# A two-block transformer layer on one core: latent attention's unrotated queries and keys made with features on partitions, and eight gate steps placed inside the attention

## The reference

```python
cq = rmsnorm_2(q_lat, q_norm_g[l])                       # 512 x 384
qb = (cq @ w_uq[l]).reshape(B, S, MLA_HEADS, MLA_QK_DIM) # 8 heads x 96
q_nope, q_rope = jnp.split(qb, [MLA_NOPE_DIM], axis=-1)  # 64 unrotated, 32 rotated
q_rope = apply_rope(q_rope, cos_b, sin_b)
ckv = rmsnorm_2(kv_lat, kv_norm_g[l])                    # 512 x 256
kvb = (ckv @ w_ukv[l]).reshape(B, S, MLA_HEADS, MLA_NOPE_DIM + MLA_V_DIM)
k_nope, vb = jnp.split(kvb, [MLA_NOPE_DIM], axis=-1)
k_rope = apply_rope(k_r[:, :, None, :], cos_b, sin_b)[:, :, 0, :]   # one 32-wide part for all heads
o_b = mla_attention(q_nope, q_rope, k_nope, k_rope, vb)  # causal softmax attention
y = sigmoid(g_a) * (o_a @ w_o_swa[l]) + sigmoid(g_b) * (o_b @ w_o_mla[l])
```

## Time and profile before

| | |
|---|---|
| median of three runs | 1228.16 us |
| the profiled execution's own time | 1228.82 us |
| its span in the trace | 1226.6 us |
| PE busy / DVE / ACT / POOL | 1203.6 / 630.9 / 542.0 / 513.6 us |
| granted TensorE clock | 0.998 of full speed |
| DMA engines' share | 28.9% |

### The profile page before, as it was taken

One profiled execution on the slowest core, in us unless ns is written; L12 is line 12 of the kernel. 1 busy time (PEld: TensorE's weight loads), 2 busy tenths in 40 slices (PEclk: granted clock), 3 DMA queues, 4 the chain that ended last, 5 costly groups with the idle time before them and its releaser, 6 DMA issues.

```text
span 1226.6 us, 15784 instructions
## 1 busy us (share of the span) xinstructions
PE 1203.6 (98%) x5888; PEld 999.9 (82%) x5888; DVE 630.9 (51%) x1489; ACT 542.0 (44%) x971; POOL 513.6 (42%) x279
## 2 busy tenths in 40 slices
PE   9999999999999999999999999999999999999997
PEld 8878788888888888699878878788888888888886
DVE  5789765774437284974855685855222231230003
ACT  6443573476523354534855476434323232231112
POOL 1428362454443424035353693443444434434441
PEclk9999999999999999999999999999999999999999
DMA  8205552202322522133012202333232332323221
GB/s 272 91 14 154 156 173 73 99 2 103 117 76 88 183 82 99 60 126 124 15 52 91 70 35 97 110 104 103 82 102 92 103 103 93 103 79 120 99 74 68
DMA packets 70842, 119.18 MB, mean 97 GB/s; under 512 B 5608, under 2 KB 33128, under 8 KB 70384
## 3 DMA queue, kind: packets, MB, share of 16 engines
q1 hardware_dynamic: 70768, 118.19, 28.9%
HBM read 107.67 MB, written 4.21 MB: 91 GB/s over the span
## 4 chain that ended last, share of the span: by engine, by line
PE 89%; DVE 4%; POOL 2%; ACT 2%; issue 1%; DMA 1%; SPq 1%; ACTq 0%; DVEq 0%; POOLq 0%
PE bank L1647 67%; PE bank L1968 9%; PE bank L1735 2%; PE bank L1703 2%; PE bank L1779 2%; PE bank L1717 2%; PE bank L1679 2%; POOL w_lo L678 1%; DVE tmp L1434 1%; PE bank L1818 1%; POOL w_lo L661 1%; ACT w_hi L781 1%; DVE xT L1436 0%; DVE sc L1183 0%; DMA w_raw<-in_w_in 0%
## 5 line engine op out<-in xcount | busy, mean ns | idle before, releaser
L661 POOL TENSOR_TENSOR w_lo<-w_raw,w_hi 128x2048 fp32r<-128x2048 f32 (+4 forms) x82 | 365.3, 4454 | 582.5 <-ACT w_hi L748 529.0
L1647 PE MATMUL bank<-aH,w_hi 128*128 128x512 f32 x800 | 318.7, 398 | 2.4 <-DVE mx L1183 0.8
L1647 PE MATMUL bank<-aH,w_lo 128*128 128x512 f32 x800 | 312.2, 390 | 0.0
L1647 PE MATMUL bank<-aL,w_hi 128*128 128x512 f32 x800 | 312.0, 390 | 0.0
L748 ACT ACTIVATE w_hi<-w_raw 128x2048 fp32r<-128x2048 f32 (+4 forms) x78 | 143.9, 1846 | 259.7 <-PE bank L1647 161.3
L1647 PEld LDWEIGHTS bank<-aH,w_hi 128*128 128x128 f32 x800 | 150.7, 188 | 32.0 <-issue 3.3
L1647 PEld LDWEIGHTS bank<-aH,w_lo 128*128 128x128 f32 x800 | 150.1, 188 | 32.2
L1647 PEld LDWEIGHTS bank<-aL,w_hi 128*128 128x128 f32 x800 | 150.6, 188 | 26.6 <-issue 0.2
L1106 DVE TENSOR_TENSOR fg<-bank,rB 128x512 f32<-128x512 f32 x22 | 15.1, 691 | 128.2 <-PE bank L1647 128.2
L1647 PE MATMUL bank<-w_hi,aH 128*128 128x512 f32 (+4 forms) x224 | 77.7, 347 | 2.2 <-ACT aH L991 1.9
L1647 PE MATMUL bank<-uH,w_hi 128*128 128x512 f32 x192 | 75.1, 391 | 1.7 <-DVE uL L1538 1.7
(11 more groups left out here) (313 smaller groups left out, 2132.7 us busy)
## 6 DMA issues: line engine op xcount, KB each, us to landing
w_raw<-in_w_in SPq DMA_DIRECT2D x23, 1024.0 KB, 4.9
w_raw<-in_w_gate SPq DMA_DIRECT2D x22, 512.0 KB, 3.6
w_raw<-in_w_up SPq DMA_DIRECT2D x22, 512.0 KB, 4.5
w_raw<-in_w_down SPq DMA_DIRECT2D x11, 1024.0 KB, 4.8
w_raw<-in_w_merge SPq DMA_DIRECT2D x8, 1024.0 KB, 4.8
w_raw<-in_w_out SPq DMA_DIRECT2D x8, 1024.0 KB, 4.9
w_raw<-in_w_ple_gate SPq DMA_DIRECT2D x4, 1024.0 KB, 4.8
w_raw<-in_w_in SPq DMA_DIRECT2D x4, 512.0 KB, 7.2
```

The lines of the kernel that those rows point to most:

```text
L661: pool.tensor_tensor(out=w_lo[:, c % 2, 0:n], in0=w_raw[:, c % 2, 0:n], in1=w_hi[:, c % 2, 0:n].bitcast(F32), op=ALU.subtract).then_inc(w_ ...
L1647: ins = pe.matmul(o, l, r, start=(kk == 0 and m == 0), stop=(kk == total - 1 and m == 2), skip_group_check=True)
```

## The change

The columns of the two weight matrices are gathered by kind instead of by group of heads. `uqn` makes the unrotated 64 features of all 8 heads with features on partitions (weights stationary, 36 matmuls of 512 columns; a bank holds two heads), `uqr` the 32 rotated ones with tokens on partitions (36 of 256 columns), `ukn` the unrotated keys with features on partitions (24 of 512), `ukv` the values (24 of 512). ACT copies the two halves of a bank of `uqn` or `ukn` to two heads of `mqT` or `mkT`. The rotated queries are turned by two groups of four transposes (`t.mq`, four heads in each), the shared rotated key by four (`t.kr`); DVE copies them to rows 64 to 96. The key's rotated rows are split once for both buffers of `mK` and stay there. DVE rotates all eight heads in one pass.

Each such weight chunk is loaded by one DMA per row block of 128, with runs of 64 floats (256 bytes) or 32 floats (128 bytes).

Eight of the 16 gate steps ahead of the attention go into it: one in every step from i = 2 to 25, then one from i = 27 and two from i = 33. ACT and POOL split the weights of `n3` at later steps. On POOL the second chunk of `n2` is split after the first two heads and no longer ahead of them.

```diff
-        unit(f"uq{i}", QR, 3, [("w_uq_2", 384 * i, 384)])
-    for i in range(2):
-        unit(f"ukv{i}", KVR, 2, [("w_ukv_2", 512 * i, 512)])
+    unit("uqn", QR, 3, [("w_uq_2", 0, DH)], H)
+    unit("uqr", QR, 3, [("w_uq_2", DH, MR)], H)
+    unit("ukn", KVR, 2, [("w_ukv_2", 0, DH)], H)
+    unit("ukv", KVR, 2, [("w_ukv_2", DH, DH)], H)
...
-SIDE_FIRST = {"fox": 8, "dsa": 8, "swa": 10, "mla": 16}
-SIDE_TAIL = {"fox": ((29, 2),), "dsa": ((29, 2),), "swa": ((25, 1), (35, 2)), "mla": ((22, 1),)}
-SIDE_HI = {"fox": (20, 27), "dsa": (20, 27), "swa": (16, 24), "mla": (11, 19)}
+SIDE_FIRST = {"fox": 8, "dsa": 8, "swa": 10, "mla": 8}
+SIDE_TAIL = {"fox": ((29, 2),), "dsa": ((29, 2),), "swa": ((25, 1), (35, 2)), "mla": ((27, 1), (33, 1))}
+SIDE_HI = {"fox": (20, 27), "dsa": (20, 27), "swa": (16, 24), "mla": (19, 27)}
...
-           "swa": ((16, 17, 18, 19), (24, 25, 26, 27)), "mla": ((12, 13, 16, 17), (20, 21, 24, 25))}
+           "swa": ((16, 17, 18, 19), (24, 25, 26, 27)), "mla": ((20, 21, 22, 23), (28, 29, 30, 31))}
...
-    for u in ("uq", "ukv"):
-        fill(f"{u}0", four); fill(f"{u}1", [4, 5, 6, 7])
-    fill("t.mq0", [0, 3, 4, 5]); fill("t.mk0", [6, 7, 0, 3])
-    fill("t.mq1", [4, 5, 6, 7]); fill("t.mk1", [0, 3, 4, 5])
+    fill("t.kr", [6]); fill("uqn", four); fill("uqr", [4, 5, 6, 7])
+    fill("ukn", four); fill("t.mq", [0, 3]); fill("ukv", [4, 5, 6, 7])
...
-                for arr, r0, c0, w, off in ps:
+                for arr, r0, c0, w, off, heads in ps:
+                    if heads > 1:
+                        for k in range(per):
+                            rows = dram[arr][0, r0 + k * P:r0 + (k + 1) * P, :].rearrange("p (h d) -> p h d", h=heads)
+                            sp_.dma_start(v[:, k, :].rearrange("p (h d) -> p h d", h=heads),
+                                          rows[:, :, c0:c0 + w]).then_inc(w_landed[c % 2], 16)
+                        continue
...
-                    t, m_ = ((mqT, mQ), (mkT, mK))[p]
+                    t, m_, n = ((mqT, mQ, MQK), (mkT, mK, DH))[p]
                     pool.wait_ge(mla_hi_ready, 2 * h + p + 1)
-                    pool.tensor_tensor(out=m_[0:MQK, h % 2, 1, :], in0=t[0:MQK, h, :],
-                                       in1=m_[0:MQK, h % 2, 0, :].bitcast(F32), op=ALU.subtract).then_inc(mla_lo_ready, 1)
+                    pool.tensor_tensor(out=m_[0:n, h % 2, 1, :], in0=t[0:n, h, :],
+                                       in1=m_[0:n, h % 2, 0, :].bitcast(F32), op=ALU.subtract).then_inc(mla_lo_ready, 1)
...
-            lo_through(UNITS["n2"][0] + 1)
+            lo_through(UNITS["n2"][0])
             for h in range(2):
                 split_head(h)
+            lo_through(UNITS["n2"][0] + 1)
             scale_rows("mla", sc2)
...
-                ahead(f"uq{i}")
-                for b in range(NB):
-                    evac(f"uq{i}", b, uq[i][:, b, :], src=bank_of(f"uq{i}", b)[:, 0:QR])
-            for i in range(2):
-                ahead(f"ukv{i}")
-                for b in range(NB):
-                    src = bank_of(f"ukv{i}", b)[:].rearrange("p (h d) -> p h d", h=4)
-                    wait_filled(act, f"ukv{i}", b)
-                    act.activation(mk[i][:, b, :, 0:DH], src[:, :, 0:DH], ACT.Copy).then_inc(mk_ready, 1)
-                    act.activation(mvS[:, b, 4 * i:4 * i + 4, 0, :], src[:, :, DH:2 * DH], ACT.Copy).then_inc(split_hi, 1)
+            for u, t in (("uqn", mqT), ("ukn", mkT)):
+                ahead(u)
+                for j in range(NB):
+                    wait_filled(act, u, j)
+                    act.activation(t[0:DH, 2 * j, :], bank_of(u, j)[0:DH, :], ACT.Copy)
+                    empties(act.activation(t[0:DH, 2 * j + 1, :], bank_of(u, j)[DH:P, :], ACT.Copy), u, j)
+                if u == "uqn":
+                    ahead("uqr")
+                    for b in range(NB):
+                        evac("uqr", b, uqR[:, b, :], src=bank_of("uqr", b)[:, 0:H * MR])
+            ahead("ukv")
+            for b in range(NB):
+                wait_filled(act, "ukv", b)
+                act.activation(mvS[:, b, :, 0, :], bank_of("ukv", b)[:].rearrange("p (h d) -> p h d", h=H),
+                               ACT.Copy).then_inc(split_hi, 1)
             hi_through(UNITS["n2"][0] + 1)
-            for i in range(2):
-                for j in range(4):
-                    evac(f"t.mk{i}", j, mkT[0:MQK, 4 * i + j, :], src=bank_of(f"t.mk{i}", j)[0:MQK, :])
-            wait_emptied(act, "t.mq1", 3)
             exps("mla", sc2, pT2, low_rows2)
...
-                    kr = kvl[:, b, KVR:KVR + MR].rearrange("p (o d) -> p o d", o=1).broadcast_to([P, 4, MR])
-                    ins = dve.tensor_copy(mk[i][:, b, :, DH:MQK], kr)
-                ins.then_inc(kr_copied, 1)
+            evac("t.kr", 0, krS[DH:MQK, :], src=bank_of("t.kr", 0)[0:MR, :])
             for j in range(NB):
                 gate_tile("n1", j, gates2[NB + j])
+            for b in range(NB):
+                wait_emptied(dve, "uqr", b)
+            rope_blocks(uqR[:, :, :].rearrange("p b (h d) -> p b h d", h=H), H, 16, "3", rp3)
+            wait_emptied(dve, "t.kr", 0)
             for i in range(2):
-                for b in range(NB):
-                    wait_emptied(dve, f"uq{i}", b)
-                uq4 = uq[i][:, :, :].rearrange("p b (h d) -> p b h d", h=4)
-                rope_blocks(uq4[:, :, :, DH:MQK], 4, 16, "3", rp3)
+                dve.tensor_copy(mK[DH:MQK, i, 0, :], krS[DH:MQK, :]).then_inc(kr_split, 1)
+            dve.wait_ge(kr_split, 2)
             for i in range(2):
-                for b in range(NB):
-                    splits[0] += 1
-                    dve.wait_ge(split_hi, splits[0])
-                    src = bank_of(f"ukv{i}", b)[:].rearrange("p (h d) -> p h d", h=4)
-                    empties(dve.tensor_tensor(out=mvS[:, b, 4 * i:4 * i + 4, 1, :], in0=src[:, :, DH:2 * DH],
-                                              in1=mvS[:, b, 4 * i:4 * i + 4, 0, :].bitcast(F32), op=ALU.subtract), f"ukv{i}", b)
-            for i in range(2):
-                for j in range(4):
-                    evac(f"t.mq{i}", j, mqT[0:MQK, 4 * i + j, :], src=bank_of(f"t.mq{i}", j)[0:MQK, :])
-                if i == 0:
-                    wait_emptied(dve, "t.mq0", 3)
-                    wait_emptied(dve, "t.mk0", 3)
-                    for h in range(2):
-                        split_head(h)
-            wait_emptied(dve, "t.mk1", 3)
+                dve.tensor_tensor(out=mK[DH:MQK, i, 1, :], in0=krS[DH:MQK, :], in1=mK[DH:MQK, i, 0, :].bitcast(F32),
+                                  op=ALU.subtract).then_inc(kr_split, 1)
+
+            def q_rope(h):
+                wait_filled(dve, "t.mq", h // 4)
+                ins = dve.tensor_copy(mqT[DH:MQK, h, :], bank_of("t.mq", h // 4)[MR * (h % 4):MR * (h % 4) + MR, :])
+                if h % 4 == 3:
+                    empties(ins, "t.mq", h // 4)
+                else:
+                    ins.then_inc(q_roped, 1)
+
+            for h in range(2):
+                q_rope(h)
+            for h in range(2):
+                dve.wait_ge(q_roped, h + 1)
+                dve.wait_ge(kr_split, 4)
+                wait_emptied(dve, "uqn", h // 2)
+                wait_emptied(dve, "ukn", h // 2)
+                split_head(h)
+            for h in range(2, H):
+                q_rope(h)
+            for b in range(NB):
+                splits[0] += 1
+                dve.wait_ge(split_hi, splits[0])
+                empties(dve.tensor_tensor(out=mvS[:, b, :, 1, :], in0=bank_of("ukv", b)[:].rearrange("p (h d) -> p h d", h=H),
+                                          in1=mvS[:, b, :, 0, :].bitcast(F32), op=ALU.subtract), "ukv", b)
+            for j in range(NB):
+                wait_emptied(dve, "ukn", j)
+            for half in range(2):
+                wait_emptied(dve, "t.mq", half)
             softmax("mla", sc2, pT2, lambda h, b: tab("causal")[:, (3 - b) * P:4 * P], low_rows2, oB)
...
-            def turn_mq(i):
-                pe.wait_ge(roped, 6 + 2 * NB + i)
-                for j in range(4):
-                    turn_tile(f"t.mq{i}", j, lambda b: uq[i][:, b, j * MQK:(j + 1) * MQK], rows=MQK)
-
-            def turn_mk(i):
-                pe.wait_ge(kr_copied, 2)
-                pe.wait_ge(mk_ready, 4 * i + 4)
-                for j in range(4):
-                    turn_tile(f"t.mk{i}", j, lambda b: mk[i][:, b, j, :], rows=MQK)
-
-            gemm("uq0", cqH, cqL, True, u_from("t.cq", 0))
-            gemm("uq1", cqH, cqL, True)
-            gemm("ukv0", ckH, ckL, True, u_from("t.ck", 0))
-            gemm("ukv1", ckH, ckL, True)
-            turn_mq(0)
-            side("mla", 0, 4)
-            turn_mk(0)
-            side("mla", 4, 8)
-            turn_mq(1)
-            side("mla", 8, 12)
-            turn_mk(1)
-            side("mla", 12, 16)
-            for j in range(4):
-                wait_emptied(pe, "t.mk1", j)
+            pe.wait_ge(roped, 5 + 2 * NB)
```

(15 more changed lines are left out.)

30 lines of the change are left out of this document (12 added, 18 removed).

## The result

The changed kernel takes 1231.39 us (median of ten runs, 1229.89 to 1232.41) against 1228.28 us of the kernel before (ten runs, 1227.17 to 1230.22): a ratio of 1.0024, 95% interval 1.0015 to 1.0033. It is slower by 3.1 us, and the forecast of 1227.0 us was wrong, with its range too (1224.0 to 1230.8).

A forecast was written before the change was run, and what follows sets the result against it. TensorE, busy 98% of the span, was taken as the bound: its program plus waits. The last value product ending 1.25 us earlier moved the end equally, 1228.16 - 1.25 = 1226.9, given as 1227.0 us, range 1224.0 to 1230.8.

The forecast's parts named there:

- TensorE's work: Latent attention stage: matmul time about unchanged (23.4 to 23.5 us), fewer transposes, so TensorE loses 5.4 us of work.
- The chain ahead of the attention: Through ACT, POOL and DVE before the attention: waits of 5.7 us replace 5.4 us of transposes; ninth gate step at 685.95.
- because of POOL: Ninth gate step, ahead of the attention: held until 685.95 by POOL's low part of n2's second chunk, ending at 685.85.
- In the attention: Ninth gate step to last value product: eleven more gate steps (7.7 us) and 2.9 us of waits; ends 1.25 us earlier.
- 2.3 for the low part of the last head ahead of step 28: Within the attention: TensorE waits 2.3 us for POOL's low part of the last head, the largest of three waits summing 2.9.
- Behind the attention: After the last value product: three fewer gate steps gain nothing, as `zb0` starts 21.0 us later; the end moves 1.25 us.
- The wait of 1.10 becomes 3.1: Ahead of `zb0`, behind the attention: TensorE has 2.0 us less to do, so its wait grows from 1.10 to 3.1 us.
- Loads: Weight DMAs in runs of 128 and 256 bytes: hidden, cost 0; upper bound 1.5 us if short runs took twice the row.
- rival (c): Small weight loads take twice the row's time and come late: 1228.4 us; part of the 61%.
- (b): Inside the attention, POOL excludes DVE, delaying its casts and maxima, and POOL gets rows later: 1230.7 us, 12%.
- (d): Gate steps put into the attention only fill time POOL's pace left empty; 5.3 us of waits stay: 1229.3 us, within 61%.

The follow-up runs named there:

- layout alone: The changed kernel with the gate-step tables and POOL's order put back as before (16 gate steps ahead of the attention), only the new query and key layout left: 1224.57 us.
- both gaps filled: The changed kernel with 27 matmuls nobody reads put into TensorE's two gaps (ahead of first scores and ninth gate step, and ahead of step 27): 1228.04 us.
- the gates alone: The kernel before, old layout with 64 transposes, given only the changed kernel's gate steps, weight halves and quarters and POOL's order: 1234.52 us.

## Why the prediction was wrong

**TensorE's work**: right, in that TensorE is busy 5.0 us less in the layout alone for the 5.4 forecast. Of these, 2.7 are gained from S to V once enough work stands behind them. The layout alone gains 4.0 us, but the other 1.3 come behind V.

**The chain ahead of the attention**: right in nearly all its links. Counted from S, POOL's first chunk ends at 26.97 us (forecast 26.8), its second at 37.57 (37.45); the waits are 0.44, 0.48, 0.73 and 2.88 + 0.78 = 3.66, for 0.5, 1.0, 0.3 and 3.9. DVE is 1.0 late at bank 4; 0.6 of this are its six copies, each of which takes 4.29 / 6 = 0.72 instead of 0.62. That is not POOL's doing: the first copy of a rotated part, at 670.99, takes 0.67 while POOL is idle. So the third score tile waits for DVE's first maximum until the very moment at which POOL's second chunk ends, and the ninth gate step, which was to start "because of POOL", starts one tile of scores later. The cast of `mQ` that was to wait for POOL took 4.11 us, until 676.52; the one of `mK` behind it 0.41. What failed is the step from the waits to the time: "waits of 0.5 + 1.0 + 0.3 + 3.9 = 5.7 us have taken the place of the 5.4 us of transposes" prices a wait at its length. The forecast had the gap right and took the work behind it at full clock. The ninth gate step starts 38.70 us from S instead of 37.55, and from the third score tile on scores and gates run at 0.52 until 693.40.

**In the attention**: the sum of waits, 2.9, was right in size (3.09), and its place wrong. The step "2.3 for the low part of the last head ahead of step 28" named the wrong consumer: the gate step of 27 came to POOL's fourth quarter first. POOL's rows and the head's low part are only the next in line, as the run with gate steps from 29 shows (1.84 and 0.34). And it was one gap, not three small waits, so the clock fell a second time.

The two falls cost 3.4 us together by the medians (both gaps filled against the changed kernel) and 1.9 each when filled apart. The traces close the sum from S to V, where 5.3 us were missed. With both gaps filled the ninth gate step starts 38.88 us from S, of which 0.69 are the fill, so 38.19 without it: 0.64 over the forecast, DVE's lateness. From there to V are 68.51 us, against 37.55 to 105.85 = 68.30 in the forecast: 0.2 over, the size of the gap. The other 4.4 us go with the clock: 3.72 that filling gives back and the 0.69 that it takes itself. No run took DVE's copies alone. Behind V, 1.7 came back that the forecast did not have, and this hid part of the miss.

**Behind the attention**: the anchor was right; `zb0` starts with the chain from the last head's bank, 19.3 us behind V in the changed kernel and with a wait of 1.45 us for DVE. "The wait of 1.10 becomes 3.1" was mis-sized, since the chain it waits for became 1.7 us shorter. From `xT`'s reload to ACT's high part of `zb0` were 11.61 us before; in the timelines of ACT and SyncE after:

```profile
761.98 0.34 SPq L638 DMA_DIRECT2D xT<-x_scratch  x1
...
772.37 1.92 ACT L753 ACTIVATE w_hi<-w_raw 128x2048 fp32r<-128x2048 f32 x1 [8.54 <-DMA w_raw<-in_w_o_mla]
```

These are 10.39. I had taken the 11.61 for a constant, and it does not look like the scatter of one execution either: in all twelve traces with the new layout this stretch takes 10.24 to 10.53, in both with the old one 11.61 and 11.22 (the gates alone). The program and the bytes of the stretch are the same in both, so why it goes with the layout stays open. Of the 1.7 us, 1.2 are this stretch; the reload also starts 1.61 us behind V with ten steps left and 2.07 with thirteen. In V to end three steps fewer gain 0.4 (469.43 against 469.79 of the layout alone), close to the nothing that was forecast.

**Loads**: right. The profile names a DMA as the releaser of no wait of TensorE in the stage; rival (c) did not come. The changed kernel's trace also has the rows that were missing, from 605 to 680 us (count, KB each, us to landing); the first has runs of 256 bytes, the second of 128:

```profile
w_raw<-in_w_uq SPq DMA_DIRECT2D x3, 256.0 KB, 3.4
w_raw<-in_w_uq SPq DMA_DIRECT2D x3, 128.0 KB, 3.3
```

So even the shortest runs took the 3.4 us of the row used and not twice as much. Half the bytes in half the run took as long, so by the byte the short runs are slower here too.

**The rivals**: (b) gave 1230.7 us, nearest to the result, but not by its mechanism. A cast takes 1.10 us at 725.75, and no later maximum is in a wait. (d) is half right: the steps in the attention are not gained, since POOL's gap stays. None held the clock, although the forecast wrote down a gap of 3.9 us and read the clock of 1.00 off the windows. The trace of before had a fall outside those windows, at 504 us; it is shown below.

## What to carry to other kernels

A wait of TensorE is not priced by its length alone: where it stands in one piece, look at the granted clock behind it in a trace of a like gap, and add what the following work loses there. Work that is taken from TensorE ahead of a chain through other engines pays only as far as other TensorE work still covers that chain: here the same new layout gains 4.0 us with 16 gate steps ahead of the attention, loses 3.1 with eight (and POOL's new order), and 12 do as well as 16 once their gap is filled. Before a chain is priced from a profile, compare one of its transfers over several executions, and do not call a difference scatter before both kernels have been looked at more than once.
